# Starting four late projections with two tiles by chunk, splitting four weight tiles ahead, adding squares on VectorE, and moving the first splits of the down projection into the up projection

## The reference, cut to what matters

```
x = x + mixer(rms_norm(x, g))        # e2: causal attention, df: differential attention
x = x + (silu(gate) * val) @ w_down  # gate, val = causal 3-tap conv of rms_norm(x, g2) @ w_up
```

## Time and profile before

| what | value |
|---|---|
| median of 3 runs | 2607.91 us |
| the profiled execution | 2608.47 us |
| its span in the trace | 2606.60 us |
| PE busy | 94% of the span |
| mean granted TensorE clock | 0.978 of full |

### The profile page before, as it was taken

The page is one execution under the profiler, slowest core; times in us unless marked ns, Lnnn a source line. Parts: engine busy times, 40 slices in busy tenths (PEclk is TensorE's granted clock), DMA queues, the critical chain, the costliest instruction groups (busy, mean ns, idle before and its releaser), DMA issues.

```text
span 2606.6 us, 32861 instructions
## 1 busy us (share of the span) xinstructions
PE 2451.5 (94%) x12608; PEld 1800.7 (69%) x12608; DVE 1125.9 (43%) x1839; ACT 968.6 (37%) x1596; POOL 345.8 (13%) x234
## 2 busy tenths in 40 slices
PE   7999899899999998999999999999989879999898
PEld 4888664366868786655776478878767654788786
DVE  4000542534442105642436256664534452566644
ACT  4111434444343425533226243332342561333323
POOL 1332001200322420001000010004310000000142
PEclk9999899999999999999999999999999999999999
DMA  7111231000131212112220122222212102222221
GB/s 293 57 65 62 97 118 49 25 32 1 52 119 57 77 61 74 50 47 81 81 81 2 50 88 97 92 93 81 97 66 87 42 1 70 84 97 95 83 96 42
DMA packets 51871, 191.67 MB, mean 74 GB/s; under 512 B 5755, under 2 KB 6139, under 8 KB 51484
## 3 DMA queue, kind: packets, MB, share of 16 engines
q1 hardware_dynamic: 51740, 189.83, 21.2%
HBM read 187.71 MB, written 2.10 MB: 73 GB/s over the span
## 4 chain that ended last, share of the span: by engine, by line
PE 84%; DVE 6%; ACT 6%; issue 2%; POOL 1%; DMA 0%; SPq 0%; ACTq 0%; DVEq 0%; POOLq 0%
PE PS L272 6%; PE PS L567 6%; PE PS L569 6%; PE PS L568 6%; PE PS L1584 5%; PE PS L1611 4%; PE PS L2195 3%; PE PS L2197 3%; PE PS L2196 3%; PE PS L1597 3%; PE PS L1291 2%; PE PS L543 2%; PE PS L544 2%; PE PS L542 2%; PE PS L891 2%
## 5 line engine op out<-in xcount | busy, mean ns | idle before, releaser
L567 PE MATMUL PS<-H_HI,W_SPLIT 128*128 128x512 f32 x704 | 279.8, 397 | 6.6 <-DVE W_SPLIT L2520 6.6
L569 PE MATMUL PS<-H_HI,W_SPLIT 128*128 128x512 f32 x704 | 278.1, 395 | 0.0
L568 PE MATMUL PS<-H_LO,W_SPLIT 128*128 128x512 f32 x704 | 277.8, 395 | 0.0
L422 ACT ACTIVATE W_SPLIT<-WT 128x1024 fp32r<-128x1024 f32 x88 | 93.0, 1059 | 299.3 <-PE PS L569 262.8
L439 POOL TENSOR_TENSOR W_SPLIT<-WT,W_SPLIT 128x1024 fp32r<-128x1024 f32 x44 | 108.6, 2471 | 611.3 <-ACT W_SPLIT L2348 611.3
L2520 DVE TENSOR_TENSOR W_SPLIT<-WT,W_SPLIT 128x1024 fp32r<-128x1024 f32 x84 | 104.7, 1248 | 166.6 <-ACT W_SPLIT L422 166.3
L272 PE MATMUL PS<-SB,WT 128*128 128x512 f32 x384 | 167.3, 598 | 5.2 <-DVE SB L1734 3.1
L2540 DVE TENSOR_TENSOR G_LO<-SB,G_HI 128x512 fp32r<-128x512 f32 x44 | 111.6, 2541 | 126.9 <-ACT G_HI L2350 126.9
L567 PEld LDWEIGHTS PS<-H_HI,W_SPLIT 128*128 128x128 f32 x704 | 132.5, 188 | 39.2 <-DVE W_SPLIT L2520 7.5
L568 PEld LDWEIGHTS PS<-H_LO,W_SPLIT 128*128 128x128 f32 x704 | 132.5, 188 | 32.2 <-issue 1.0
L2195 PE MATMUL PS<-G_HI,W_SPLIT 128*128 128x512 f32 x352 | 140.7, 400 | 14.6 <-DVE G_LO L2540 14.6
(11 more groups left out here) (309 smaller groups left out, 5211.0 us busy)
## 6 DMA issues: line engine op xcount, KB each, us to landing
WT<-weights SPq DMA_DIRECT2D x316, 512.0 KB, 3.6
SB<-weights SPq DMA_DIRECT2D x13, 512.0 KB, 13.0
SB<-rpb SPq DMA_DIRECT2D x8, 512.0 KB, 4.7
HT<-rpb SPq DMA_DIRECT2D x8, 512.0 KB, 4.3
XT<-tokens SPq DMA_DIRECT2D x4, 768.0 KB, 7.0
out<-HT SPq DMA_DIRECT2D x4, 512.0 KB, 2.6
SB<-late SPq DMA_DIRECT2D x1, 1280.0 KB, 5.7
SB<-con SPq DMA_DIRECT2D x1, 1248.0 KB
```

The source lines that it names most:

```text
L567: pe.matmul(PS[:, s, :], hi, H_HI[:, c, :], start=(c == 0), stop=False)
L568: pe.matmul(PS[:, s, :], hi, H_LO[:, c, :], start=False, stop=False)
L569: last = pe.matmul(PS[:, s, :], lo, H_HI[:, c, :], start=False, stop=(c == KC - 1))
```

## The change

`W_EARLY`, two more split buffers, holds weight tiles 0 and 1 of each late projection, so tiles 0 to 3 can all be split before the projection starts (`split_of`); from tile 4 on two buffers serve as before. PE runs tiles 0 and 1 together (`first_two_pe`): chunk c of tile 0, then chunk c - 1 of tile 1. The sum of squares is added on VectorE behind the residuals (`late_sum_dve`), and GpSimd's part goes. The matmul of ones moves from before tile 3 to before tile 4, the Ln and Exp of late_rs from before to behind the split of tile 4, the column factor of the qkv projections to before the split of tile 5, the copies of qkv tiles 0 and 1 behind late_rs, and the scaling in `up` begins one step later (`scaled_by`). The first two splits of `down`, of weights and of `G`, are written into the last steps of `up` on ScalarE and VectorE, and PE's first tile of `down` waits bank by bank and takes the banks in the order 4 to 7, 0 to 3.

```diff
+        W_EARLY = over("W_EARLY", "SB", BIG + 4096, [128, 2, 2, TILE])
+        def split_of(t):
+            return W_EARLY[:, t] if t < 2 else W_SPLIT[:, t % 2]
...
-        def late_sum_pool(g, name):
+        def late_sum_dve(v, name):
...
         def scaled_by(t):
-            return max(0, min(t - 1, 2 * (t - 3)))
+            return max(0, min(t - 1, 2 * (t - 4)))
...
                 t = 8 * q + s if isinstance(q, int) else None
-                if t == 2:
+                if t == 0:
+                    before(act)
+                if t == 4:
                     late_hi_act(act, name)
                     late_squares_act(act, name)
+                act.wait_ge(sem(f"w_ready{slot}"), (rnd + 1) * 16)
+                if t is None or t >= 4:
+                    act.wait_ge(sem("tile_used"), q * 8 + (g0 + s - 1))
+                dst = W_SPLIT[:, s % 2] if t is None else split_of(t)
+                act.activation(dst[:, 0, :], W[:, slot, :], ACT.Copy).then_inc(sem("w_hi"), 1)
                 if t == 4:
                     late_rs_act(act, name)
...
             if take:
-                for t in range(n - 3, n):
-                    take(t // 8, t % 8)
+                take((n - 3) // 8, (n - 3) % 8)
+                for k in range(2):
+                    down_split(act, name, k)
+                    take((n - 2 + k) // 8, (n - 2 + k) % 8)
+        def down_split(act, name, k):
+            l = int(name[2])
+            at = FIRST_TILE[f"down{l}"] + k
+            act.wait_ge(sem("acted"), FC * l + k + 1)
+            act.activation(G_HI[:, k, :], G[:, k, :], ACT.Copy).then_inc(sem("g_hi"), 1)
+            act.wait_ge(sem(f"w_ready{at % SLOTS}"), (at // SLOTS + 1) * 16)
+            act.wait_ge(sem("tile_used"), at - 1)
+            act.activation(W_SPLIT[:, k, 0, :], W[:, at % SLOTS, :], ACT.Copy).then_inc(sem("w_hi"), 1)
...
+        def first_two_pe(pe, name, banks_free):
+            h0, low0 = split_at[name][0], low_at[name]
+            pe.wait_ge(sem("w_low"), low0 + 2)
+            for k in range(KC + 1):
+                for t in range(2):
+                    c = k - t
+                    if not 0 <= c < KC:
+                        continue
+                    if c == 0:
+                        pe.wait_ge(sem("evac_dve"), banks_free + t + 1)
+                    if t == 0:
+                        pe.wait_ge(sem("h_lo"), h0 + c + 1)
+                    hi, lo = (W_EARLY[:, t, x, c * 128:c * 128 + 128] for x in range(2))
+                    pe.matmul(PS[:, t, :], hi, H_HI[:, c, :], start=(c == 0), stop=False)
+                    pe.matmul(PS[:, t, :], hi, H_LO[:, c, :], start=False, stop=False)
+                    last = pe.matmul(PS[:, t, :], lo, H_HI[:, c, :], start=False, stop=(c == KC - 1))
...
             def act(self, act, before=None):
+                if before:
+                    before(act)
                 for t in range(26):
-                    if t == (1 if self.early else 2):
+                    if t == (3 if self.early else 4):
                         late_hi_act(act, self.name)
-                    if t == 2:
+                    if t == 4:
                         late_squares_act(act, self.name)
+                    if t < 24:
+                        act.wait_ge(sem(f"w_ready{(self.g0 + t) % SLOTS}"), ((self.g0 + t) // SLOTS + 1) * 16)
+                        if t >= 4:
+                            act.wait_ge(sem("tile_used"), self.g0 + t - 1)
+                        elif self.early and t >= 2:
+                            act.wait_ge(sem("tile_used"), self.g0 + t - 3)
+                        act.activation(split_of(t)[:, 0, :], W[:, (self.g0 + t) % SLOTS, :], ACT.Copy).then_inc(sem("w_hi"), 1)
                     if t == 4:
                         late_rs_act(act, self.name)
+                    if t == 5:
                         act.wait_ge(sem("col_summed"), self.k + 1)
...
+                    if t == 4:
+                        for k in range(2):
+                            act.wait_ge(sem("tile_used"), self.g0 + k + 1)
+                            act.activation(QKE[:, k, :], PS[:, k % 6, :], ACT.Copy).then_inc(sem("qk_raw"), 1)
...
             def dve(self, v, add):
-                self.low(v, 0)
-                if not self.early:
-                    self.low(v, 1)
+                for t in range(3 if self.early else 4):
+                    self.low(v, t)
                 residual_split_dve(v, self.name, add)
                 if self.early:
-                    self.low(v, 1)
-                for t in range(2, 24):
+                    self.low(v, 3)
+                late_sum_dve(v, self.name)
+                for t in range(4, 24):
...
                 project_split_pe(pe, f"up{l}")
-                wait_projected(pe, f"up{l}")
...
-                    for n in range(8):
+                    for n in [4, 5, 6, 7, 0, 1, 2, 3] if first else range(8):
+                        if first:
+                            pe.wait_ge(sem("evac_dve"), d0 + 36 + (n + 4) % 8 + 1)
...
                 for t in range(2 * FC - 2, 2 * FC + 1):
                     if t < 2 * FC:
                         scaled(t // 8, t % 8)
                     conv((t - 1) // 8, (t - 1) % 8)
+                    if t < 2 * FC:
+                        low_g(0, t - 2 * FC + 2)
```

More of the change, by code:

```diff
@@ L368, in late_sum_pool @@
             for c in range(1, KC):
-                g.wait_ge(sem("squared"), c0 + c + 1)
+                v.wait_ge(sem("squared"), c0 + c + 1)
                 if c > 1:
-                    g.wait_ge(sem("sq_taken"), k + c)
-                g.tensor_tensor(XSUM, XSQ[0] if c == 1 else XSUM, XSQ[c % 2], ALU.add).then_inc(sem("sq_taken"), 2 if c == 1 else 1)
+                    v.wait_ge(sem("sq_taken"), k + c)
+                v.tensor_tensor(XSUM, XSQ[0] if c == 1 else XSUM, XSQ[c % 2], ALU.add).then_inc(sem("sq_taken"), 2 if c == 1 else 1)
         def late_sum_pe(pe, name):
@@ L546, in project_halves_pe @@
             tiles(name, n, body)(pe)
+        def first_two_pe(pe, name, banks_free):
[14 more added lines that the diff above has]
+                    last = pe.matmul(PS[:, t, :], lo, H_HI[:, c, :], start=False, stop=(c == KC - 1))
+                    if c == KC - 1:
+                        last.then_inc(sem("tile_used"), 1)
         def project_split_pe(pe, name):
@@ L555, in body @@
                 t = 8 * q + s if isinstance(q, int) else None
-                if t == 3:
+                if t == 0:
+                    first_two_pe(pe, name, d0 - 8)
+                if t is not None and t < 2:
+                    return
+                if t == 4:
                     late_sum_pe(pe, name)
@@ L563, in body @@
                 for c in range(KC):
-                    if isinstance(q, int) and 8 * q + s == 0:
-                        pe.wait_ge(sem("h_lo"), h0 + c + 1)
                     hi, lo = (W_SPLIT[:, s % 2, k, c * 128:c * 128 + 128] for k in range(2))
@@ L706, in pe @@
                 pe.wait_ge(sem("evac_act"), after(self.prev)[0])
-                for t in range(24):
-                    slot = (self.g0 + t) % SLOTS
-                    if t == 3:
+                first_two_pe(pe, self.name, self.d0 - 8)
+                for t in range(2, 24):
+                    if t == 4:
                         late_sum_pe(pe, self.name)
@@ L773, in act @@
                         act.activation(self.RC, self.RC, ACT.Exp, scale=-0.5).then_inc(sem("rc_ready"), 1)
[L774 to L780, removed]
+                    if t < 4:
+                        continue
+                    if t == 4:
+                        for k in range(2):
+                            act.wait_ge(sem("tile_used"), self.g0 + k + 1)
+                            act.activation(QKE[:, k, :], PS[:, k % 6, :], ACT.Copy).then_inc(sem("qk_raw"), 1)
                     k = t - 2
@@ L2039, in _ @@
             window.pool(g)
-            late_sum_pool(g, "e2_in")
-            late_sum_pool(g, "up0")
             split_w_pool(g, "down0")
-            late_sum_pool(g, "df_in")
-            late_sum_pool(g, "up1")
             split_w_pool(g, "down1")
@@ L2185, in ffn_pe @@
                 project_split_pe(pe, f"up{l}")
-                wait_projected(pe, f"up{l}")
+                d0 = ev_base[f"up{l}"][1]
                 def body(q, s, rnd, slot):
@@ L2344, in down @@
                 def down(q, s, rnd, slot):
+                    if isinstance(q, int) and 8 * q + s < 2:
+                        return
                     act.wait_ge(sem(f"w_ready{slot}"), (rnd + 1) * 16)
@@ L2506, in conv, with low_g @@
                         v.tensor_tensor(G[:, q * 4 + s // 2, :], a, SG[:, (s // 2) % 2, :], ALU.mult).then_inc(sem("acted"), 1)
+                def low_g(q, s):
+                    v.wait_ge(sem("g_hi"), q * 8 + (FC * l + s + 1))
+                    v.tensor_tensor(G_LO[:, s % 2, :], G[:, q * 8 + s, :], G_HI[:, s % 2, :].bitcast(F32), ALU.subtract)\
```

(16 more changed lines are left out.)

15 lines of the change are left out of this document (4 added, 11 removed).

## The result

The changed kernel takes 2559.65 us (median of 4 runs, 2557.63 to 2561.76) against 2606.66 us for the kernel before (4 runs, 2605.19 to 2609.98). The ratio is 0.9818, interval 0.9801 to 0.9835. I had forecast 2569.4 with a range of 2563 to 2579. The time is gained where the prediction said, but the two qkv projections (e2_in and df_in) gained some 3 us more each, and PE's clock did not fall in any late projection.

The account below looks back on a forecast made before the run. PE, busy 94% of the span, was taken as the bound, losing time only in waits and slow stretches. Gains of 3.6 + 5.1 + 3.2 + 10.7 + 9.3 + 8.6, less 2, made 38.5 us: median 2569.4, range 2563 to 2579.

Parts of the forecast that it names:

- e2_in and df_in: Starts of both qkv projections: a 2.65 us wait before tile 5 replaces 1.57 before tile 4; gains 3.2 and 10.7 us.
- R: In each late projection, the start of PE's matmul of ones, from which the prediction counts later times.
- Clock after the new waits: Before tile 5 of e2_in and df_in: each clock fall costs 0 to 2 us, taken as 1 each, 2 us back.
- The price of a matmul: Late projections: 0.232 us each, 5.57 per tile of 24, 22.29 for four tiles; 0.17 to 0.2 more at low clock.
- up0, up1: Starts of the two up projections: 3.6 and 5.1 us gained, with no wait before tile 5.
- df_in's two-tile start: Start of df_in: the residual chain decides; two tiles together need 1.39 us per chunk against its 1.26, so no waiting.
- up to down: From up to down, both layers: 9.3 and 8.6 us gained; PE starts at T + 0.3 if conv steps stall beside GpSimd.
- T: The end of up in each layer, from which the prediction times the start of down.
- the starts of `down` (1): Rival, start of down: waits stay partly open, up to 9.8 us over two layers, 2572 to 2579; chance 0.12.
- "the clock stays up everywhere" (2): Rival: no clock fall after the waits before tile 5, both down starts closed, 2566 to 2567; chance 0.13.
- The start that fails to take effect (3): Rival: reordering has no effect at one start, for instance df_in, giving back some 6 us, 2576; chance 0.04.
- A fall of the clock before tile 5 (4): Rival, qkv projections: clock falls and stays low through both, 178 us, 2747, slower than before; chance 0.03.

## Why the prediction was wrong where it was

- **The failed step** is in "e2_in and df_in": "then the column Ln and Exp ... split 5 at R + 8.2". The split comes first, at R + 5.0. PE starts tile 5 at R + 7.77, close to my R + 7.9 for PE being ready by itself, so the "wait of 2.65 us before tile 5" does not exist. That is 2.8 us in each of two projections, 5.6 together. The run with that order shows the wait where the prediction had it, tile 5 at R + 10.55.
- **Clock after the new waits**: 2 us taken off for waits that did not exist; the stretches show 1.00. These two points are 7.6 of the 8.7 us by which the sum was short of the span's 47.2. The rest is 0.4 to 0.5 us in each of the e2 and df sections, less than their attention differs between runs, and 0.3 in down0, less 0.4 at the start.
- **The price of a matmul, R and the first four tiles**: right to 0.15 us in all four (22.68, 22.67, 22.35 and 22.68 against 22.69, 22.69, 22.49 and 22.69).
- **up0, up1**: right (10.8 and 12.3 against 10.75 and 12.25 with the start of `down`). VectorE's denser tiles 5 to 7 cost PE nothing: no idle mark.
- **df_in's two-tile start**: right, and alone worth 3.1 us.
- **up to down**: right. I had put PE's start at T + 0.3; it is T + 0.24 (1744.00 against 1743.53 + 0.23). The open point was whether VectorE's conv steps stand still beside GpSimd: a conv step that takes 0.75 us alone takes 2.79 while GpSimd's split runs (1739.77 and 1739.59), so the dearer bound was the true one. The Trainium skill, SBUF — State Buffer, "SBUF: two separate sides", says that a VectorE operation with two SBUF inputs and a GpSimd operation lock each other out of a shared pair of ports for a whole instruction, whichever starts first going first. The trace agrees: GpSimd starts 0.18 us earlier and keeps its 2.43 us.
- **The rivals**: the starts of `down` (1) closed. The conditions of "the clock stays up everywhere" (2) were both met, but its time of 2566 to 2567 kept the wait before tile 5 and so was 6 to 7 us too long as well. The start that fails to take effect (3) did not occur. A fall of the clock before tile 5 (4) was seen only in the run made for that wait, for 1.56 us in one projection, and did not last. Its price of a matmul at the lower level was read a little narrow: 3.4 us for 9 and 4.8 for 11 are 0.38 and 0.44 us each, not 0.40 to 0.43; nothing else rests on it.
- **The range** failed because its low end came from the same misread order. It took in the clock and rounding, but no case in which that wait was absent; a wait that the change adds deserved a case without it.

## What to carry to other kernels

When a step moves in a hand-written queue, write out the new order of that engine line by line from the code before giving it times: here the durations of this chain were right to 0.2 us and the order of two steps cost 5.6 us. Give a new wait that you have derived a case in which it is not there. And when several edits attack one wait, try each alone: moving the adds to VectorE gave 18.1 us of span alone and nothing measurable beside the four tiles split ahead.

## What the runs showed that I had not expected

- One edit, the adds of squares on VectorE, removed all of the wait before tile 2 in three projections, since ScalarE may write a square only when the adder has taken the one two before it (`sq_taken`, two buffers), and so the adder's pace set that of ScalarE's queue. In up0 the eight squares take 6.5 us with VectorE and 9.7 with GpSimd, though they are 0.6 us each.
- The same wait of 2.22 us was followed by the low clock in one projection (0.70 over 5.7 us) and not in the other (1.00). Before the change a wait of 3.30 us was not followed by it in up0, but one of 3.29 was in up1 (0.50 from 2223.60 on). The stretch behind the one in up0:

```profile
1518.50:1523.00 4.50, 4.45 (x19) 3.66 (x20) 1.13 (x1) 0.00 (x1) 0.00 (x0) 1.00 0.02 4
```

  So the length of the wait alone does not tell. Of one wait under 2.5 us the cost of the clock can only be given as 0 or 1.5 to 2 us; the prediction had set the fall by the length of the wait.
- The same code's span differed by 6.2 us between two profiled executions with all late projections alike to 0.2 us. The attention of df can differ in the same way, between two runs whose code is alike there: granted clock 0.91 in the changed kernel and 0.95 in the one that waits for all of `up`.

```profile
2000.00:2117.00 117.00, 95.06 (x514) 66.73 (x512) 64.11 (x246) 68.91 (x191) 0.00 (x0) 0.91 0.05 18
```

```profile
2000.00:2115.00 115.00, 92.15 (x515) 63.44 (x514) 64.49 (x246) 68.62 (x191) 0.00 (x0) 0.95 0.06 18
```

The first is the changed kernel, the second the other, whose df section is 3.6 us shorter though nothing in it was edited. That the clock makes the difference is argued from these stretches and not tested.
